# A fused decoder block on one core: u rows of 64 instead of 32 tokens fetched by gathers, the dense u products cut from 352 to 320 columns

## The reference

```python
def _peer(h, w_q, subkeys, u, v):          # 512 tokens, D=1024, 128*128 experts
    q = (xb @ w_q).reshape(TOK, 8, 2, 128)
    s = einsum('thcd,hcnd->thcn', q, subkeys)
    sv, si = top_k(s, 16)                  # 16 of 128 keys on each side
    top_s, pos = top_k(sv[..0,:,None] + sv[..1,None,:], 16)
    idx = (si0 * 128 + si1)[pos]           # 16 experts for each of 8 heads
    g = softmax(top_s)
    a = gelu(einsum('td,thkd->thk', xb, u[idx]))
    return einsum('thk,thkd->td', g * a, v[idx])
```

## Time and profile before

| what | value |
|---|---|
| median of 3 runs | 1557.44 us (1556.79 to 1559.13) |
| span of the profiled execution | 1555.2 us |
| TensorE clock granted | 1.0 throughout |
| busy share PE / DVE / ACT / POOL | 100% / 82% / 45% / 49% |
| moved by the DMAs | 385.44 MB, 248 GB/s over the span |

### The profile page before, as it was taken

One profiled execution on the slowest core, in us unless ns is written; L12 is line 12 of the kernel. 1 busy time (PEld: TensorE's weight loads), 2 busy tenths in 40 slices (PEclk: granted clock), 3 DMA queues, 4 the chain that ended last, 5 costly groups with the idle time before them and its releaser, 6 DMA issues.

```text
span 1555.2 us, 25687 instructions
## 1 busy us (share of the span) xinstructions
PE 1548.0 (100%) x9433; PEld 1377.8 (89%) x9433; DVE 1278.6 (82%) x2548; ACT 695.2 (45%) x1012; POOL 755.9 (49%) x484
## 2 busy tenths in 40 slices
PE   9999999999999999999999999999999999999998
PEld 9987877888889999999989898999999999888887
DVE  5898675836899799999588787878888888888887
ACT  6333565444343477777333333333343433333334
POOL 4675444434566566653255455555545455322220
PEclk9999999999999999999999999999999999999999
DMA  4222122433224489998899999999999989989994
GB/s 165 96 95 74 64 68 95 140 124 130 85 88 139 147 274 324 316 333 268 295 381 357 342 340 345 341 348 339 348 345 343 354 329 334 323 308 315 331 322 148
DMA packets 151730, 385.44 MB, mean 248 GB/s; under 512 B 11872, under 2 KB 61536, under 8 KB 151520
## 3 DMA queue, kind: packets, MB, share of 16 engines
q1 hardware_dynamic: 59328, 203.13, 36.7%
q0 software_dynamic: 41472, 151.01, 26.8%
q10 hardware_dynamic: 50848, 30.30, 6.6%
HBM read 355.03 MB, written 28.84 MB: 247 GB/s over the span
## 4 chain that ended last, share of the span: by engine, by line
PE 90%; DVE 9%; ACT 0%; issue 0%; POOL 0%; ACTq 0%; POOLq 0%
PE ps L2226 32%; PE ps L2069 26%; PE ps L1748 6%; PE ps L1811 5%; PE ps L2087 5%; PE ps L1975 3%; DVE hot_w L1632 3%; DVE rows L1571 2%; PE ps L1710 2%; PE ps L1988 1%; DVE hot_l L1628 1%; DVE hot_l L1633 1%; DVE hot_l L1629 1%; PE ps L2212 1%; PE ps L2150 1%; PE ps L1756 1%
## 5 line engine op out<-in xcount | busy, mean ns | idle before, releaser
L2069 PE MATMUL ps<-hThi,uwhi 128*128 128x352 f32 x1024 | 330.1, 326 | 0.0
L2069 PE MATMUL ps<-hTlo,uwhi 128*128 128x352 f32 x1024 | 327.8, 322 | 0.0
L1021 ACT ACTIVATE vwhi<-vraw 128x1024 fp32r<-128x1024 f32 x128 | 135.8, 1061 | 406.9 <-PE ps L2226 347.2
L686 POOL DMA_INDIRECT rows<-in_v,gidx x128 | 165.8, 1296 | 248.6 <-DVE acc L1587 232.4
L686 POOL DMA_INDIRECT rows<-in_u,gidx x128 | 188.8, 1475 | 182.9 <-DVE rows L1580 138.8
L1546 DVE TENSOR_TENSOR vwlo<-vraw,vwhi 128x1024 fp32r<-128x1024 f32 x128 | 156.5, 1222 | 111.2 <-ACT vwhi L1021 85.9
L975 ACT ACTIVATE uwhi<-uraw 128x1024 fp32r<-128x1024 f32 x127 | 134.3, 1058 | 170.0 <-PE ps L2069 131.0
L2069 PEld LDWEIGHTS ps<-hTlo,uwhi 128*128 128x128 f32 x1024 | 192.6, 188 | 1.6
L2069 PEld LDWEIGHTS ps<-hThi,uwhi 128*128 128x128 f32 x1024 | 192.1, 188 | 1.9 <-issue 0.3
L2069 PE MATMUL ps<-hThi,uwlo 128*128 128x352 f32 x1024 | 184.0, 322 | 0.0
L2226 PE MATMUL ps<-vwhi,awhi 128*128 128x512 f32 x720 | 183.7, 390 | 0.0
(11 more groups left out here) (382 smaller groups left out, 2956.9 us busy)
## 6 DMA issues: line engine op xcount, KB each, us to landing
vraw<-in_v SPq DMA_DIRECT2D x128, 512.0 KB
uraw<-in_uT SPq DMA_DIRECT2D x127, 512.0 KB
raw<-in_wstream SPq DMA_DIRECT2D x70, 512.0 KB, 3.4
gmat<-gates_dram SPq DMA_DIRECT2D x64, 384.0 KB
gates_dram<-piece ACTq DMA_DIRECT2D x11, 2048.0 KB
xt<-in_xT SPq DMA_DIRECT2D x8, 264.0 KB, 4.8
acc<-in_x ACTq DMA_DIRECT2D x4, 512.0 KB, 4.4
rows<-in_u,gidx POOLq DMA_INDIRECT x128
```

What stands on the lines that cost most here:

```text
L686: pool.indirect_dma_start(out=rows[n % SLOTS][:], out_offset=None, in_=u if q < P else v, in_offset=bass.IndirectOffsetOnAxis(ap=gidx[:, q ...
L1021: act.activation(vw["hi"][:, m % 2, :], vraw[:, m % 2, :], ACT.Copy).then_inc(S["v_hi"], 1)
L2069: ins = pe.matmul(ps[:, k, 0:UCOLS], u_weights(a, k, far)[:, c * P:(c + 1) * P], hT[b][:, c, P + EXTRA:TOK], start=i == 0, stop=i == len(U ...
```

## The change

`EXTRA` becomes 64. The dense u products have 320 columns, and 64 gathers with 64 `item_x` take the place of 32. The quarters of the partitions hold the same tokens as before, once for tokens 0 to 31 and once for 32 to 63 (`x_`). `NMAIN` becomes 40 and the batches for gathered tokens (`XBATCH`) 8. The 64 items are spread over the first 36 batches. `U_TOP` is 22, and `LAG` 70, so that the pair stage has 58 steps and 70 v blocks come after it. The pairs of batch and fill come from a table: 38 blocks in 40 batches, then 4 in 8, and the loop of TensorE is unrolled. The reserve for the descriptors of GpSimd's DMAs is cut from 16 KB to 8 KB of each partition, and six activations are kept there.

```diff
-EXTRA = GT
+EXTRA = 2 * GT
...
-FILL = (5, 5, 6)
-GROUP = len(FILL)
-U_TOP = 20
-LAG = 56
-NGROUP = NMAIN // GROUP
-U_FILL = 2 * NGROUP + 1
-LOOPED = 4
+PRODUCTS = 3 * DC
+U_TOP = 22
+LAG = 70
+U_FILL = 38
+X_FILL = 4
 NPAIR = NK - LAG
...
-    paired = ITEMS_FIRST + (45 * min(m, NPAIR) + 15) // 16
-    return min(ITEMS, paired + max(m - NPAIR, 0))
+    return min(ITEMS, ITEMS_FIRST + (46 * min(m, NPAIR) + 22 * max(m - NPAIR, 0) + 15) // 16)
...
-    return min(EXTRA, 4 * batch // 5)
+    return min(EXTRA, EXTRA * batch // (NMAIN - 4))
+def filled(batches):
+    main, last = min(batches, NMAIN), max(batches - NMAIN, 0)
+    return 3 * (PRODUCTS * U_FILL * main // (3 * NMAIN)) + 3 * (PRODUCTS * X_FILL * last // (3 * XBATCH))
+def blocks_filled(batches):
+    return U_TOP + filled(batches) // PRODUCTS
+def batches_ahead(n):
+    return next(b for b in range(NBATCH + 1) if filled(b) >= PRODUCTS * (n - U_TOP))
...
-            for f in range(U_BY_POOL - U_TOP - 1):
-                while ahead < EXTRA + SLOTS and ahead - SLOTS < extra_before(min(NMAIN, f // 2 * GROUP + f % 2 + 1)):
+            for n in range(U_TOP + 1, U_BY_POOL):
+                beside = batches_ahead(n) if n < U_TOP + U_FILL else NMAIN
+                while ahead < EXTRA + SLOTS and ahead - SLOTS < extra_before(min(NMAIN, beside - 1)):
...
-                u_split(U_TOP + 1 + f, extra_before(batch_beside(f)))
+                u_split(n, extra_before(beside))
...
-            for g in range(QUAD):
-                ins = dve.scalar_tensor_tensor(out=gidx_x[g * GT:(g + 1) * GT, 0:GT], in0=tile1(ei, g), scalar=float(NK),
-                                               in1=tile1(ej, g), op0=ALU.mult, op1=ALU.add)
+            for x_ in range(XP):
+                for g in range(QUAD):
+                    ins = dve.scalar_tensor_tensor(out=gidx_x[g * GT:(g + 1) * GT, x_ * GT:(x_ + 1) * GT], in0=tile1(ei, x_, g),
+                                                   scalar=float(NK), in1=tile1(ej, x_, g), op0=ALU.mult, op1=ALU.add)
...
-            gate_groups(0, 0, LOOPED)
-            with pe.Fori(1, NGROUP // LOOPED, 1) as it:
-                gate_groups(it, 0, LOOPED)
-            gate_groups(0, NGROUP // LOOPED * LOOPED, NGROUP)
-
-            for batch in range(NMAIN - 2, NBATCH):
+            for batch in range(NBATCH):
...
                 gate_batch(batch, batch)
-                for i in range(batch % 2 * 12, batch % 2 * 12 + 12):
-                    u_product(n, n % 2, i)
-            for n in range(U_TOP + U_FILL + XBATCH // 2, LAG):
+                for product in range(filled(batch), filled(batch + 1)):
+                    k, i = divmod(product, PRODUCTS)
+                    u_product(U_TOP + k, (U_TOP + k) % 2, i)
+            for n in range(blocks_filled(NBATCH), LAG):
                 u_block(n, n % 2)
...
-    nc = bacc.Bacc("TRN2", target_bir_lowering=False, num_devices=1)
+    nc = bacc.Bacc("TRN2", target_bir_lowering=False, num_devices=1, dynamic_dma_scratch_size=8192)
```

More of the change, by code:

```diff
@@ L1006, in gelu @@
                     act.wait_ge(S["prod_ok"], n - LAG + 1)
-                act.activation(stored_act(n), tokens_in_pieces(ps[:, n % 2, 0:UCOLS]), ACT.Gelu).then_inc(S["gelu_ok"], 1)
+                own = stored_act(n)
+                act.activation(own, ps[:, n % 2, 0:UCOLS].rearrange("p (c t) -> p c t", t=own.shape[-1]), ACT.Gelu
+                               ).then_inc(S["gelu_ok"], 1)
             def squares(tt):
@@ L1093, in _ @@
                     v_split(0)
-                u_split(n + 2, n % 2)
-                gelu(n)
-                f = n - (U_TOP + U_FILL - 1)
-                for batch in range(min(NMAIN + 2 * f, NBATCH), min(NMAIN + 2 * f + 2, NBATCH)):
-                    gates_out(batch)
+                block_done(n)
                 if n == LAG - 2:
@@ L1468, in _ @@
             chain.done(ins)
-            dve.wait_ge(S["ynx_in"], 16 * QUAD)
+            dve.wait_ge(S["ynx_in"], 16 * QUAD * XP)
             bests = best[:].rearrange("p t h k -> p (t h) k")
@@ L1558, in weigh @@
                 dve.tensor_copy(own[:, 0:XP], gmat[:, g % 2, 0:XP, m % GRP, :])
-                dve.tensor_tensor(own[:, XP:NPIECE], stored_act(m), gmat[:, g % 2, XP:NPIECE, m % GRP, :],
-                                  ALU.mult).then_inc(S["prod_ok"], 1)
+                stored_ = stored_act(m)
+                dve.tensor_tensor(split_as(own[:, XP:NPIECE], stored_), in_pieces(stored_),
+                                  split_as(gmat[:, g % 2, XP:NPIECE, m % GRP, :], stored_), ALU.mult).then_inc(S["prod_ok"], 1)
             def weight_lo(m):
@@ L1570, in item_x @@
                 dve.wait_ge(row_in[q % SLOTS], q // SLOTS * 16 + 16)
-                dve.scalar_tensor_tensor(out=row[:], in0=row[:], scalar=1.0, in1=ynat_x[:, 0, :], op0=ALU.mult,
+                dve.scalar_tensor_tensor(out=row[:], in0=row[:], scalar=1.0, in1=ynat_x[:, q // GT, :], op0=ALU.mult,
                                          op1=ALU.mult, accum_out=dots_x[:, q:q + 1]).then_inc(S["item_ok"], 1)
@@ L1641, in _ @@
                     dve.wait_ge(S["wx_gelu"], 1)
-                    own = pick_x[0:GT, :]
-                    chain.done(dve.tensor_tensor(own, own, gate[0:GT, 1].rearrange("p h k -> p (h k)"), ALU.mult))
+                    own = pick_x[0:EXTRA, :]
+                    chain.done(dve.tensor_tensor(own, own, gate[0:EXTRA, 1].rearrange("p h k -> p (h k)"), ALU.mult))
                     chain.done(dve.tensor_copy(tab_x[:, 0], own))
@@ L2152, in gate_batch @@
                     ins.then_inc(S["g_mm"], 1)
-            def gate_groups(it, first, last):
-                for own in range(first * GROUP, last * GROUP):
-                    group, s = divmod(own, GROUP)
-                    gate_batch(it * (LOOPED * GROUP) + own, own)
-                    for product in range(3 * sum(FILL[:s]), 3 * sum(FILL[:s + 1])):
-                        k, i = divmod(product, len(U_ORDER))
-                        u_product(it * (2 * LOOPED) + (U_TOP + 2 * group + k), k, i)
-            pe.wait_ge(S["gidx_ok"], 1)
-            gate_groups(0, 0, LOOPED)
-            with pe.Fori(1, NGROUP // LOOPED, 1) as it:
-                gate_groups(it, 0, LOOPED)
-            gate_groups(0, NGROUP // LOOPED * LOOPED, NGROUP)
-            for batch in range(NMAIN - 2, NBATCH):
-                n = U_TOP + U_FILL - 1 + (batch - (NMAIN - 2)) // 2
+            pe.wait_ge(S["gidx_ok"], 1)
+            for batch in range(NBATCH):
                 if batch == NMAIN - 1:
```

65 lines of the change are left out of this document (36 added, 29 removed).

## The result

The changed kernel takes 1591.51 us (median of 5 runs, 1584.71 to 1594.19); the kernel before, measured beside it, took 1557.56 (median of 5, 1556.79 to 1559.13). The ratio is 1.021 with an interval of 1.0196 to 1.0224: slower by 2.1%, where I had forecast 1% faster. The profiled execution is the fastest of the five: 1584.71 us, span 1583.0 against 1555.2 before. The median lies 6.8 us above that execution; before, the scatter was 2 us.

What follows compares the result with a forecast made beforehand. It took TensorE and VectorE as both full in the one-hot stage, DMA engines nearly so, TensorE full in the pair stage. From 1555.2, products save 41, the one-hot stage returns some 22, DMAs 4: span 1540, median 1541; range 1522 to 1560.

Steps and rivals of the forecast that it cites:

- I take 5.5 us a batch: One-hot stage: 36 batches at 5.5 us each, from VectorE's 5.03 and the transfers' 5.75; bounds 5.1 to 6.0.
- Two buffers for v level this out (bounds: nothing, to 0.5 us on each of 23 blocks): V blocks: two buffers even out VectorE's 4.5 and 3.3 us blocks, so 70 blocks take 285 us, 4.07 each.
- I add 4 us (0 to 15): Allowance of 4 us for loads that come late here and there, giving a span of 1540.
- What costs nothing: ... the four more small DMAs: Four more small DMAs on ScalarE cost nothing, as it has 41 us left in the one-hot stage.
- 19 u blocks of 3.55 us: Ahead of the one-hot stage: 19 u blocks of 3.55 us instead of 17 of 3.87, 1.7 us later.
- Cost of a u product: Pair stage: a 320-column product takes 145.2 ns instead of 158.5; at most 41 us saved over 3072 products.
- Rival 4: Products do not shrink and stay at 158.5 ns: 30 us more, 1571 us; chance 0.03.
- Collisions: One-hot stage: VectorE dot products lose 0.25 us each when a GpSimd operation begins just before them.
- Rival 3: Transfers bound all three stages at 327, 351 and 329 GB/s: 47 us more, 1588; chance 0.13 for above 1560.
- Rival 2: Only VectorE bounds the one-hot stage, 5.1 us a batch, no load late: 1524 us (1518 to 1531); chance 0.25.
- my 538: Start of the one-hot stage: VectorE's first one-hot operation at 538 us, where it stood at 535.87 before.

Runs made afterwards that it cites:

- E1: Changed kernel, each x gather bringing 2 KB a partition instead of 4, each dot product done as two of 512 columns: 1572.51 us.
- e3: Changed kernel, GpSimd issuing the gathers for freed row buffers, all but the last, before the low part: 1575.63 us.
- e6: Changed kernel, each 2 MB store of gates split into four of 0.5 MB, one issued behind each batch: 1575.72 us.
- e8: Changed kernel with half rows (2 KB a partition) and the gathers issued ahead of the low part: 1561.21 us.
- e13: Changed kernel: gathers first, gate stores except the last in quarters, y-row copies moved, `U_TOP` 20, items over 38 batches, four v buffers: 1541.02 us, ratio to before 0.9901.
- e2: Changed kernel, the 64 dot products of gathered tokens taken over 128 of 1024 columns, gathers whole: 1575.9 us.
- E4: Changed kernel without the v gathers past the pair stage, the items running on what lies in the buffers: 1574.89 us.
- e14: Changed kernel with four raw buffers instead of two for v blocks past the pair stage, same bytes: 1567.85 us.
- e7: Changed kernel: gathers first, `U_TOP` 20, second four y-row copies moved behind a later store, 50/16 and 19/16 items a step: 1569.55 us, ratio 1.0075.
- e5: Changed kernel with 20 u blocks ahead of the one-hot stage and 40 in it, instead of 22 and 38: 1585.57 us.
- e11: Changed kernel: gathers first, gate stores in quarters, y-row copies moved, `U_TOP` 20, items over 38 batches: 1559.9 us, ratio to before 1.0014.

## Why the prediction was wrong, by its own steps

**"I take 5.5 us a batch": the step that failed.** I made it from VectorE's work and the transfers' bytes, each as a sum by itself, and took the longer with some collisions. It measured 6.04, just above my upper bound of 6.0, and 19.5 us are lost. What was missing is a third sum, the time round one row buffer: the wait for the item, GpSimd's low part of 2.4 us ahead of the issue, the landing of 6.5 us on the median and up to 10.9, and the item itself. With four buffers and 1.78 items a batch a buffer comes round once in 4/1.78 = 2.25 batches, 12.4 us at 5.5; before, it was once in 5 batches, some 20 us. By the chain at 736.14, 2.4+0.2+10.9+1.2 = 14.7 us do not fit into 12.4; with the median of 6.5 it is 10.3, which does. So it fails at the late rows: beside the stores' bursts and behind low parts. E1, e3 and e6 each take part of the waits away (to 16.4, 15.2 and 21.6), e8 nearly all, and e13 nearly all (5.8) with no byte less, though its items are spread over 38 batches. VectorE's own work is not the bound: e2 takes 1.5 us of it out of a batch and gains 0.4.

**"Two buffers for v level this out (bounds: nothing, to 0.5 us on each of 23 blocks)" and "I add 4 us (0 to 15)".** I had asked only whether VectorE's uneven items and the bytes would fit. Each loss, 14 us, was inside a bound, and the value taken was the wrong end. It is 0.2 us a block on the mean, as loads landed 1.8 us later than without gathers (5.3 against 3.5), but not evenly: from 1378 to 1438 us TensorE lost nothing, and one late load, 7.7 us from 1532.45 on, cost 4.9 us by itself, 2.9 of idling and the rest in products at the lower clock behind it. E4 and e14 show the cause. The same error as in the batch: throughput was priced, latency was not.

**"What costs nothing: ... the four more small DMAs".** I covered them with ScalarE's idle time in the one-hot stage. They are issued in the query stage, where a high part for TensorE stands behind them: 2.9 us, of which e7 gives back 2.5. **"19 u blocks of 3.55 us"**: the refill of the two u buffers sets 3.7 us; some 3 us more. That part is read off the chain. In e5 the first one-hot operation came 7.6 us earlier for two blocks less, where 3.7 us a block make 7.4 and 3.55 make 7.1; that does not decide it.

**Cost of a u product.** Right: 146.7 ns against 145.2. Rival 4 is dead. The 1.5 ns over the pair stage's 58x24 products are 2.1 us of the 3.5 that the stage lost; 1.4 us are TensorE's idle time in its window (442.57 of 444).

**Collisions.** Right in kind, too high in size: I had 0.25 us for each dot product, 16 us in all; the mean is 1277 ns where VectorE waits, so 3.6 us. They return when the waits go: 1364 ns in e3, 1434 in e11, 1438 in e13. They make most of what a cured batch has above VectorE's work: with 64/38 = 1.68 items, 3.0+1.92 of work, 0.37 of longer dot products and 5.8/38 = 0.15 of waits are 5.44 us, and e13's 38 batches take 5.47.

**Rival 3, "the transfers become the bound in all three stages", gave 1588**, 3 us from the median and 5 from the span. The number is near and the mechanism is not what the runs show. The pair stage was at 359 GB/s over 444 us, above the 351 that the rival took as an end, and lost 3 us where it had 14.5. The v blocks ran at full speed once they had buffers, at 363 GB/s while gathers were issued (e14), where the rival had 329. Only in the one-hot stage is it half right: fewer bytes do make the rows land sooner (e1). But with the loop cured e13 moves 348 GB/s at a share of 1.01, so the 327 of the rival was no limit; whether one is near, no run shows. The 327 stands in none of the rows that I gave. It is the steady part of that stage in the kernel before:

```profile
560.00:700.00 140.00, 140.00 (x1398) 135.44 (x1396) 139.61 (x226) 104.14 (x117) 86.50 (x51) 1.00 0.99 327
```

The share of 0.94 that I argued with the earlier trace rows is a mean with the stage's quiet start in it; from 560 us on the transfers already had 0.99 in the kernel before. The Trainium skill (DMA: Bandwidth & Descriptors, Where 436 GB/s comes from) gives 358 GB/s as HBM's limit for one core. The 359 of the pair stage lie at it, and e14's 363 over 242 us of v blocks above it, with TensorE full or nearly so in both. So here the measurement decides: a limit, if there is one for this mix, lies at 363 or higher, and neither stage was held back by it.

**"Rival 2: for it: 408 GB/s were reached"** carried a chance of 0.25. A window of 10 us said nothing on rows that must land in time.

**Would the forecast have held without the loop?** E13 measures 1541.02, my number for the change as it stood. That is partly luck: its one-hot stage begins at 532.8, 5 us ahead of my 538, and spreads the items over 38 batches. But the pair stage (444 against 440), the v blocks (285.6 against 285) and a batch of 5.4 to 5.5 are near the terms of my sum.

**Open.** What a fifth or sixth row buffer would do: no run tried it. The 4.5 us between the last item and the pair stage: the waits of this stretch (VectorE 5.2 us for the turned table) are read, not tested. What each piece of TensorE's lowered clock costs: it stands beside TensorE's waits for VectorE, and no run separates the two. And why the changed kernel's runs scatter over nearly 10 us; e13's scatter is 5.5, and a loop that depends on landing times would do that, but no run separates it.

## What to carry to other kernels

When transfers are added to a stage whose DMA share is already high (0.94 here on the mean, 0.99 in its steady part), add up the time round one buffer (wait, issue, landing under load, use) and divide by the number of buffers, beside the bytes and the engines' work. The landing time is the term that grows, and the late ones count, not the median: 6.5 us fitted here, 10.9 did not. Where it does not fit, look for depth before you cut bytes (the buffers of a stage that has ended), issue the gather before the work that stands ahead of it, and break up long stores, but not those behind which another engine's work stands. A DMA that is issued from a computing engine's queue cost that engine's time where it was issued (2.9 us for four on ScalarE), so price it by the stage in which it stands.

## What the runs showed of the hardware

- The same load of 512 KB landed in 3.5 us on the median over the v blocks without gathers beside it (share 0.56, 186 GB/s) and in 5.3 with them (0.91, 334); an x gather in 6.5 (4.4 to 10.9), a 2 MB store in 17.1 us.
- Rates: 363 GB/s over 242 us at a share of 0.97 (e14), 359 over 444 us at 0.96, and 348 over 207 us at 1.01. The same share is thus not the same rate. The queues differ too: for each per cent of the engines' time the loads of q1, 3.4 KB a packet, moved 5.5 MB, and q10, mostly gates at 0.6 KB, 4.6 MB.
- Issuing a small DMA took ScalarE 0.7 us, and four more of them 2.9.
- The granted clock fell where TensorE had waited for one-hot operations: 24 small products took 2.74 us at 753.90, right behind 4.9 us of waiting, and 1.39 at full clock. 2.74 and 1.39 are the two levels, 1.2 and 2.4 GHz; the granted clock of that stretch is 0.50. TensorE idled 5.65 and 4.9 us of the 20 in the two short windows shown above.

```profile
753.90:757.00 3.10, 3.10 (x26) 3.10 (x27) 3.10 (x6) 1.41 (x2) 2.31 (x3) 0.50 0.75 255
```
